# A first expert's tokens gathered as a transposed product, with bias products and tables in other places

## The reference, cut to what matters

```python
h = layer_norm(DEEPNORM_ALPHA * h + t, ln_g[i, 0], ln_b[i, 0])
# moe_ffn(h):
logits = (xt @ w_router + b_router).astype(jnp.float32)
top_logit, top_e = lax.top_k(logits, TOP_K)          # 4 of 32 experts
gate = jax.nn.softmax(top_logit, axis=-1)
...
h = xb @ w_gu[e] + b_gu[e]                           # per expert, on its tokens
h_gate, h_up = jnp.split(h, 2, axis=-1)
act = h_gate * jax.nn.sigmoid(SWIGLU_ALPHA * h_gate) * (h_up + 1.0)
return act @ w_down[e] + b_down[e]
```

## Time and profile before

| | us |
|---|---|
| runs of the kernel | 1381.45, 1381.24, 1382.12 |
| the profiled execution's own time | 1380.81 |
| its span, first to last instruction | 1379.0 |
| PE busy | 1334.6 |
| DVE busy | 441.3 |
| ACT busy | 346.8 |
| mean granted TensorE clock | 0.990 |

### The profile page before, as it was taken

The page is one execution under the profiler, slowest core; times in us unless marked ns, Lnnn a source line. Parts: engine busy times, 40 slices in busy tenths (PEclk is TensorE's granted clock), DMA queues, the critical chain, the costliest instruction groups (busy, mean ns, idle before and its releaser), DMA issues.

```text
span 1379.0 us, 17054 instructions
## 1 busy us (share of the span) xinstructions
PE 1334.6 (97%) x7358; PEld 719.0 (52%) x7358; DVE 441.3 (32%) x746; ACT 346.8 (25%) x576; POOL 48.6 (4%) x58
## 2 busy tenths in 40 slices
PE   9999999999999999969999999999999999999997
PEld 7996333333333333313333333333336998999986
DVE  5565121111111111011111110111116776878853
ACT  4441011101101110000011010110116545666642
POOL 2010000000000000000000000000002000022200
PEclk9999999999999999979999999999999999999999
DMA  9768999999999999999999999999996444265530
GB/s 376 315 236 356 424 423 429 431 430 431 430 431 430 431 430 431 431 430 429 431 431 431 429 431 432 430 429 432 430 428 271 153 153 153 79 258 184 184 122 31
DMA packets 44346, 484.17 MB, mean 351 GB/s; under 512 B 4748, under 2 KB 4800, under 8 KB 13680
## 3 DMA queue, kind: packets, MB, share of 16 engines
q1 hardware_dynamic: 42432, 477.63, 83.2%
q0 software_dynamic: 1840, 5.44, 1.1%
HBM read 481.99 MB, written 1.06 MB: 350 GB/s over the span
## 4 chain that ended last, share of the span: by engine, by line
PE 83%; DMA 11%; DVE 3%; issue 1%; ACT 1%; DVEq 0%; SPq 0%; ACTq 0%
PE bank L832 27%; PE bank L638 18%; PE bank L840 13%; DMA ring<-in_moe_w_gate_up 8%; PE bank L1140 4%; PE bank L852 4%; PE bank L805 4%; PE bank L621 3%; PE bank L824 2%; DMA ring<-in_w_in 2%; PE bank L748 2%; PE bank L1076 1%; PE bank L1026 1%; DMA arena<-in_x_by_feature 1%; DVE w_split L1549 1%
## 5 line engine op out<-in xcount | busy, mean ns | idle before, releaser
L832 PE MATMUL bank<-ring,arena 128*64 128x512 f32 x2032 | 448.2, 597 | 9.7 <-DMA ring<-in_moe_w_gate_up 9.6
L832 PEld LDWEIGHTS bank<-ring,arena 128*64 128x64 f32 x2032 | 142.5, 137 | 314.0 <-issue 291.2
L1747 DVE TENSOR_SCALAR arena<-bank 128x512 f32<-128x512 f32 x32 | 22.1, 692 | 658.6 <-PE bank L832 658.6
L840 PE MATMUL bank<-ring,arena 128*64 128x512 f32 x1024 | 227.0, 595 | 2.4 <-DMA ring<-in_moe_w_down 2.0
L638 PE MATMUL bank<-x_hi,w_split 128*128 128x256 f32 x1056 | 193.7, 284 | 2.1 <-DVE x_lo L1556 2.1
L638 PEld LDWEIGHTS bank<-x_hi,w_split 128*128 128x128 f32 x1056 | 165.9, 192 | 2.6 <-DVE x_lo L1556 1.5
L1549 DVE TENSOR_TENSOR w_split<-ring,w_split 128x2048 fp32r<-128x2048 f32 x61 | 139.5, 2290 | 60.3 <-ACT w_split L1195 60.1
L638 PE MATMUL bank<-x_lo,w_split 128*128 128x256 f32 x528 | 149.4, 283 | 0.0
L1296 ACT ACTIVATE arena<-arena 128x512 f32<-128x512 f32 x32 | 20.2, 630 | 498.8 <-DVE arena L1747 498.8
L840 PEld LDWEIGHTS bank<-ring,arena 128*64 128x64 f32 x1024 | 70.8, 137 | 137.9 <-issue 128.8
L1195 ACT CAST w_split<-ring 128x2048 fp32r<-128x2048 f32 x62 | 118.2, 1909 | 74.0 <-PE bank L638 42.5
(11 more groups left out here) (292 smaller groups left out, 1104.5 us busy)
## 6 DMA issues: line engine op xcount, KB each, us to landing
ring<-in_moe_w_gate_up SPq DMA_DIRECT2D x127, 2048.0 KB, 29.3
ring<-in_moe_w_down SPq DMA_DIRECT2D x64, 2048.0 KB, 30.3
ring<-in_ffn_w_up SPq DMA_DIRECT2D x22, 1024.0 KB, 4.8
ring<-in_w_in SPq DMA_DIRECT2D x14, 1024.0 KB, 8.1
ring<-in_ffn_w_down SPq DMA_DIRECT2D x11, 1024.0 KB, 4.8
ring<-in_a_w_in SPq DMA_DIRECT2D x10, 1024.0 KB, 20.8
ring<-in_a_w_out SPq DMA_DIRECT2D x2, 2048.0 KB, 13.8
ring<-in_w_out SPq DMA_DIRECT2D x4, 1024.0 KB, 5.0
```

What stands on the lines that cost most here:

```text
L832: last = mm(bank[q // 2][half * 64:half * 64 + 64, :], chunk(xeT, c), w[:, c % 2, q * 512:(q + 1) * 512], start=False, stop=c == KC - 1)
L840: last = mm(bank[3][half * 64:half * 64 + 64, :], chunk(actT, c), w[:, c % 4, half * 512:(half + 1) * 512], start=c == 0, stop=c == KC - 1)
```

## The change

- OUT_BANKS puts one half of the attention output in bank 7 instead of bank 0; the router's and the rank counts' results move to banks 4 and 5. Banks 0 and 1 are then free early.
- `add_bias` of the first expert runs right behind the first tile's router product. `bias_sel` for it is made before the layer norm.
- h1 is written and announced in halves of 512 columns.
- The first expert's tokens are gathered with h1 as the stationary operand (`gather_first`): eight products 64 columns wide for each tile, whose result is already transposed. The first copy of ACT and the four transposes go. The part of tile 0 runs when tile 0 is chosen and ranked, that of tile 1 after its own choice.
- The table transposes (`tables`) move behind the first weight piece.
- Of the four fillers behind the first router product one is left, and one of 256 columns is new.

```diff
-        OUT_BANKS = (4, 6, 5, 0)
+        OUT_BANKS = (4, 6, 5, 7)
...
+            def gather_first(t):
+
+                for c in range(KC):
+                    start = c // 2 * 256 + c % 2
+                    last = mm(bank[2][:, c % 4 * P + c // 4 * 64:c % 4 * P + c // 4 * 64 + 64], h1[:, t, start:start + 255:2],
+                              sel[:, t, :], start=t == 0 and c == 0, stop=t == NT - 1, skip_group_check=True)
+                return last
+
             for t in range(NT):
-                pe.wait_ge(h1_ready, t + 1)
                 for g in range(2):
+                    pe.wait_ge(h1_ready, 2 * t + g + 1)
...
                 if t:
+                    pe.wait_ge(chosen_ready, 1)
+                    mm(RANKS[0], before, chosen[:, 0, :], start=True, stop=True).then_inc(rank_ps, 1)
+                    pe.wait_ge(h1T_dve, 1)
+                else:
                     repeat(3, 1)
-                    pe.wait_ge(h1T_dve, 1)
+                    pe.wait_ge(moe_small_in, 4 * 16)
...
                 if t == 0:
+                    pe.wait_ge(bsel_ready, 1)
+                    add_bias()
                     repeat(3, 1)
 
-            pe.wait_ge(chosen_ready, 1)
-            mm(bank[0][:, 0:N_EXP], before, chosen[:, 0, :], start=True, stop=True)
-            mm(bank[0][:, N_EXP:2 * N_EXP], ones, chosen[:, 0, :], start=True, stop=False)
-            repeat(3, 1)
+            pe.wait_ge(sel_ready, 1)
+            gather_first(0)
+            mm(bank[3][:, 0:T], ident, cst[:, 0:T], start=True, stop=True)
+            mm(RANKS[1], ones, chosen[:, 0, :], start=True, stop=False)
             pe.wait_ge(chosen_ready, 2)
...
-            repeat(3, 1)
+            mm(RANKS[1], before, chosen[:, 1, :], start=False, stop=True).then_inc(rank_ps, 1)
+            pe.wait_ge(sel_ready, 2)
+            gather_first(1).then_inc(xeT_ps, 1)
...
-            pe.wait_ge(sel_ready, 1)
-            gather().then_inc(xe_ps, 1)
...
-            pe.wait_ge(xe_ready, 1)
-            turn_chunks(2, xe, 2).then_inc(xeT_ps, 1)
...
                     gate_up(s, buffer_of(n, 2)).then_inc(piece_done, 1)
+                    if i == 0 and s == 0:
+                        tables()
...
-            act.wait_ge(xe_ps, 1)
-            copy(xe, bank[2][:, :]).then_inc(xe_ready, 1)
...
+                for g in range(2):
+                    cols = slice(g * 512, (g + 1) * 512)
+                    stt(h1[:, t, cols], h1[:, t, cols], r, row_b[:, cols], ALU.mult, ALU.add).then_inc(h1_ready, 1)
+            places = const("slot")
+
+            def first_places(t):
+
+                dve.wait_ge(rank_ps, t + 1)
+                link(stt(place[:, t, :], RANKS[t], 0.5, chosen[:, t, :], ALU.add, ALU.mult))
+                ts(sel[:, t, :], places[:, 0:CAP], place[:, t, 0:1], None, ALU.is_equal).then_inc(sel_ready, 1)
```

More of the change, by code:

```diff
@@ L164, in build @@
         LEVEL_BANKS = (4, 6, 7, 4, 5, 6, 7, 4)
-        OUT_BANKS = (4, 6, 5, 0)
+        OUT_BANKS = (4, 6, 5, 7)
+        LOGITS = [bank[4][:, t * N_EXP:(t + 1) * N_EXP] for t in range(NT)]
+        RANKS = [bank[5][:, t * N_EXP:(t + 1) * N_EXP] for t in range(NT)]
         OUT_ORDER = (3, 0, 1, 2)
@@ L191, in build @@
         selgT = at(3456, NT, P)
-        bias_sel = at(3712, CAP, rows=64)
+        bias_sel = at(13548, CAP, rows=64)
         actT = at(6144, 4, P)
@@ L772, in _, with add_bias @@
             before = const("before")
+            def add_bias():
+                for half in range(2):
+                    for q in range(2):
+                        rows = slice(q * 32, q * 32 + 32)
+                        mm(bank[q][half * 64:half * 64 + 64, :], bias_sel[rows, :], bgu[rows, half, :],
+                           start=True, stop=False)
+            def gather_first(t):
[4 more added lines that the diff above has]
+                return last
             for t in range(NT):
-                pe.wait_ge(h1_ready, t + 1)
                 for g in range(2):
+                    pe.wait_ge(h1_ready, 2 * t + g + 1)
                     b = 4 + 2 * t + g
@@ L818, in chunk @@
                 return v[:, c % 4, (c // 4) * 64:(c // 4) * 64 + 64]
[L820 to L825, removed]
             def gate_up(s, w):
@@ L854, in scatter, with tables @@
                 return last
-            pe.wait_ge(sel_ready, 1)
-            gather().then_inc(xe_ps, 1)
[L858 to L861, removed]
-                turn(bank[3][0:N_EXP, T + t * P:T + (t + 1) * P], place[:, t, :])
-            for t in range(NT):
-                last = mm(bank[4][0:N_EXP, 0:1], chosen[:, t, :], ones[:, 0:1], start=t == 0, stop=t == NT - 1)
-            last.then_inc(table_ps, 1)
-            pe.wait_ge(xe_ready, 1)
-            turn_chunks(2, xe, 2).then_inc(xeT_ps, 1)
+            def tables():
+                pe.wait_ge(gates_ready, 1)
+                for t in range(NT):
+                    turn(bank[3][0:N_EXP, t * P:(t + 1) * P], gates[:, t, :])
+                for t in range(NT):
+                    turn(bank[3][0:N_EXP, T + t * P:T + (t + 1) * P], place[:, t, :])
+                for t in range(NT):
+                    last = mm(bank[4][0:N_EXP, 0:1], chosen[:, t, :], ones[:, 0:1], start=t == 0, stop=t == NT - 1)
+                last.then_inc(table_ps, 1)
             def put_down(i):
@@ L1653, in choose @@
                 dve.wait_ge(logit_ps, t + 1)
-                link(tt(logit[:, t, :], bank[1 + t][:, 0:N_EXP], br, ALU.add))
+                link(tt(logit[:, t, :], LOGITS[t], br, ALU.add))
                 link(dve.max(top8[:, t, :], logit[:, t, :]))
@@ L1664, in choose, with select_bias @@
                                   ALU.add).then_inc(chosen_ready, 1)
+            def select_bias(i):
+                ts(bias_sel, ones[0:64, 0:CAP], const("own")[0:64, i:i + 1], None, ALU.mult).then_inc(bsel_ready, 1)
+            select_bias(0)
             for t in range(NT):
@@ L1676, in _ @@
                 r = refine(t)
-                stt(h1[:, t, :], h1[:, t, :], r, row_b, ALU.mult, ALU.add).then_inc(h1_ready, 1)
+                for g in range(2):
[6 more added lines that the diff above has]
+                ts(sel[:, t, :], places[:, 0:CAP], place[:, t, 0:1], None, ALU.is_equal).then_inc(sel_ready, 1)
             choose(0)
@@ L1680, in _ @@
             dve.tensor_copy(h1T[:, 4:8, P:T], bank[7][:, :].rearrange("p (c n) -> p c n", c=4)).then_inc(h1T_dve, 1)
+            first_places(0)
             choose(1)
             dve.wait_ge(chosen_ready, 2)
-            places = const("slot")
+            first_places(1)
             def select(i):
@@ L1688, in select @@
                    place[:, :, i:i + 1].to_broadcast([P, NT, CAP]), ALU.is_equal).then_inc(sel_ready, 1)
-            def select_bias(i):
-                ts(bias_sel, ones[0:64, 0:CAP], const("own")[0:64, i:i + 1], None, ALU.mult).then_inc(bsel_ready, 1)
             def weigh(i):
@@ L1697, in weigh @@
                 last.then_inc(selg_ready, 1)
-            dve.wait_ge(rank_ps, 1)
-            link(stt(place.rearrange("p t e -> p (t e)"), bank[0][:, 0:2 * N_EXP], 0.5,
-                chosen.rearrange("p t e -> p (t e)"), ALU.add, ALU.mult))
-            select(0)
             dve.wait_ge(gexp_ready, 1)
@@ L1732, in _ @@
                 if i + 1 < N_EXP and not pause:
-                    dve.wait_ge(xe_ps, i + 1)
+                    dve.wait_ge(*((xe_ps, i) if i else (xeT_ps, 1)))
                     select(i + 1)
```

24 lines of the change are left out of this document (10 added, 14 removed).

## The result

The changed kernel takes 1385.51 us (median of 7 runs, 1383.07 to 1386.85), the kernel before 1381.38 (7 runs, 1380.89 to 1382.83). The ratio is 1.0026, 95% interval [1.0017, 1.0036]: 4.1 us slower, 0.3%. The forecast was 1387.0 with a range of 1380.2 to 1390.5.

What follows compares the result with a forecast made beforehand. The full DMA stream of weights, whose head waits for PE, was taken as the bound. The middle, +5.6, of +7.4 and +3.7 on 1380.81 gave 1386.4, and 0.6 for the runs 1387.0; range 1380.2 to 1390.5.

Steps and rivals of the forecast that it cites:

- What bounds the kernel: MoE: the full DMA weight stream sets the end; its head waits for PE's first weight piece, us for us.
- The room: Stream's head: piece 11 lands 8.1 us after issue, a lone piece 7.5, so 0.6 us of lateness is free.
- 1.5 us of room cover it: Tables behind the first weight piece: 0.8 us of PE, covered by piece 20's landing 9.0 after issue against 7.5.
- Up to the clock's fall nothing moves.: PE up to tile 0's router product: same list as before, so the clock falls as before, at about 119.2.
- a later fall: Clock falls at 125, behind tile 1's router product: first weight piece done at 141.0, +4.3, stream +3.7.
- the middle, +5.6: End of the kernel: the forecast taken between +7.4 (early fall) and +3.7 (later fall).
- The first branch: Clock falls at about 119.2 and stays at 1.2 GHz well into the expert products: piece +8.0, stream +7.4.
- The upper end of the range: 1390.5 us: the early fall with the narrow products at double price, +8.6, and 0.6 for the runs.
- The narrow products at 1.2 GHz: Router product and gather_first on PE: 3.2 us per sixteen instead of 1.80, by the transposes' ratio 1.81 / 1.03.
- The rival that they keep their time: Narrow products bound by loads do not slow with the clock: +3.2 or 1.0, 1382.5 to 1384.7; chance 0.10.
- The strides: gather_first loads h1 with a stride of two: at most 0.9 us more per batch of 16, taken as 0.
- The gain of an early first piece: Stream's head: an earlier first weight piece only closes the dip from 360 to 430 GB/s, at most 0.8 us.

Runs made afterwards that it cites:

- a_hotlate: a_hot with the tables behind the third weight piece of the first expert instead of the first: 1382.03 us, ratio 0.9992.
- b_nofill: The kernel before without its two fillers around the rank products: 1382.74 us, ratio 1.0017.
- b_delay: The kernel before with five more fillers of 512 columns ahead of the first expert's gather: 1385.29 us, ratio 1.0031.
- b_narrow: The kernel before with both gather_first in place of the old gather, ACT's copy and the transposes, nothing else: 1382.76 us, ratio 1.0007.
- b_first: The kernel before with one more filler, ahead of tile 0's router product: 1381.44 us, ratio 1.0005.
- a_again: The changed kernel once more, unaltered: 1385.84 us, ratio 1.0025 to the kernel before.
- a_nofirst: The changed kernel without its filler ahead of tile 0's router product: 1387.33 us, ratio 1.005 to the kernel before.
- a_fill: The changed kernel with three full fillers where PE would wait, one replacing the 256-column one: 1383.98 us, ratio 1.0024 to the kernel before.
- a_wide: The changed kernel with the old wide gather, ACT's copy and four transposes instead of both gather_first: 1384.76 us, ratio 1.0022 to the kernel before.
- a_hot: a_fill plus a full filler ahead of gather_first(0) and a 256-column one ahead of tile 1's router product: 1381.86 us, ratio 1.001.
- a_latetab: The changed kernel with the tables behind the first expert's third weight piece instead of the first: 1384.88 us, ratio 1.0018 to the kernel before.
- a_midlate: a_hotlate without the 256-column filler ahead of tile 1's router product: 1383.19 us, ratio 1.0012 to the kernel before.

## Why the prediction was right

Right in its result and mostly in its mechanism; one premise and two sizes were wrong.

**What bounds the kernel.** Right. Over the 14 profiled executions the second layer's first load is issued a nearly fixed time behind piece 12: 869.03 us in the kernel before (1009.18 less 140.15), and 868.8 to 869.6 in all but one. The exception is a_hotlate at 870.95, whose piece 11 took 10.0 us to land, and the trace doesn't show why. So up to that load what counts is when PE releases the slots of pieces 11 and 12. From its issue to the end of the execution it was 370.7 to 372.3 us, and 372.9 to 373.3 in the four executions with the fall in the second layer. In the table all times are in us, and the lateness is against the kernel before.

| profiled execution | filler ahead of tile 0's router product | clock at 1.2 GHz, 115 to 145 | piece 11 late | second layer's first load late |
|---|---|---|---|---|
| kernel before | no | 119.2 to 122.6 | | |
| b_nofill | no | 127.7 to 131.1 | 0.84 | 0.95 |
| b_delay | no | 125.7 to 129.2 | 4.88 | 4.74 |
| b_narrow | no | never | 0.48 | 0.34 |
| b_first | yes | 125.1 to 128.5 | 0.22 | 0.27 |
| changed kernel | yes | 126.2 to 139.9 | 4.05 | 5.12 |
| a_again | yes | 126.4 to 140.1 | 3.99 | 4.68 |
| a_nofirst | no | 120.3 to 123.8, 127.2 to 140.8 | 5.57 | 6.63 |
| a_fill | yes | never | -1.05 | 0.35 |
| a_wide | yes | 120.5 to 124.0, 127.4 to 141.0 | 5.32 | 6.75 |
| a_hot | yes | never | 0.05 | 1.34 |
| a_latetab | yes | 126.7 to 140.4 | 4.26 | 4.52 |
| a_hotlate | yes | 122.1 to 125.5 | 2.67 | 4.59 |
| a_midlate | yes | 125.8 to 142.9 | 8.04 | 8.41 |

**The room.** The prediction took 0.6 us of room at piece 11 and 1.5 us for the tables. Both came from comparing a landing time with that of a lone piece, 7.5 us. That holds for the first late piece only. The piece behind it lands 9.1 to 9.3 after its issue in all the kernels whose stream had run dry (9.3 after, 9.1 in b_delay and b_nofill); the piece ahead had not landed when it was issued (148.26 against 145.10 after). In the kernel before piece 12 took 9.5 (140.15 to 149.65): by that its room was 0.2 to 0.4, and in the loads not even this is to be seen, as they are as late as piece 12 within about 0.5 in all traces but a_hotlate's. The tables, placed exactly ahead of it, cost their 0.9. The step "1.5 us of room cover it" failed, because it looked at piece 20. The 0.8 named there as their price past the cover was close.

**"Up to the clock's fall nothing moves."** This step failed twice. A filler had been added ahead of tile 0's router product, so the list was not the same. And the place of the fall does not repeat even where it is: b_nofill, b_delay and b_narrow have the kernel before's own list up to 125, and their clock fell at 127.7, at 125.7 and never. Of the five executions without the filler two have an early fall, of the nine with it a_wide and a_hotlate. So the traces don't show that the filler put it off. The prediction was a middle of two branches, +7.4 and +3.7. The changed kernel is the second, "a later fall": issue of piece 11 predicted at 141.0, measured 140.76; stream +3.7, measured +5.1: the tables add 0.9, the missing room 0.6, a piece 11 a little earlier than forecast takes 0.25 off, and the rest is open. Even the 141.0 is in part two errors that cancel: the second `gather_first` started at 129.96, about 1.1 earlier than the sum has it, as the clock fell only inside the first, and from there to the end of the weight piece it took about 0.9 more. That the middle, +5.6, came close to +4.1 to +4.9 is partly luck: the branch that took place, with the room and the tables as forecast, gives 1385.1, and the two terms that it lacks happen to be about what the middle adds. The first branch, one fall from 119 into the expert products, is in no trace: where the clock fell that early, in four executions, it was back after 3.4 to 3.5 us. The upper end of the range does not follow from its terms either: 1380.81 + 8.6 + 0.6 is 1390.0, not 1390.5.

**The narrow products at 1.2 GHz.** The forecast was 3.2 us for sixteen, measured 3.68 with the end of the last one. From their start to the next instruction's, as the 1.80 was read that it comes from, they took 3.31 in a_midlate (134.01 to 137.32). Their weight loads, by groups at 2.4 and at 1.2 GHz:

```profile
L808 PEld LDWEIGHTS bank<-arena 128*128 128x128 f32 x16 | 1.9, 191 | 0.8 <-issue 0.8
...
L788 PEld LDWEIGHTS bank<-arena 128*128 128x128 f32 x16 | 3.5, 328 | 0.8 <-DVE arena L1705 0.8
```

The mean load goes from 191 to 328 ns, a ratio of 1.72 beside the 1.76 of the transposes. The rival that they keep their time falls. By the rule quoted from the Trainium skill ("TensorE: Matmul & The Clock Gate", LDWEIGHTS) such a load would take 107 ns, an estimate from its 128 columns, with no word of the clock. The trace disagrees at both clocks.

**The strides.** Taken at 0, and nothing more is to be seen: at 2.4 GHz in a_fill sixteen strided products took 1.92 us from their start to the next instruction's (125.00 to 126.92), in the same trace sixteen contiguous ones, half as wide, 1.87 (117.44 to 119.31).

**The gain of an early first piece.** It was capped at 0.8. In a_fill piece 11 went out 1.05 early, the stream ran at 436 instead of 360 GB/s from 135 to 140 and at 397 instead of 442 from 140 to 145, with piece 12 held back by the tables. Piece 12 went out at 140.00, 0.15 early, and the second layer's first load was not earlier (1009.53). So an early piece 11 gave nothing in this execution, while piece 12 was not early too.

**Why the clock stays down.** That fillers can give the loss back is shown: a_hot, with five more and all the other edits in place, keeps the clock in its profiled execution and gives back 3.3 of the 4.65 us of the median. Three (a_fill) and four (a_midlate, with its tables late) gave back less, 2.0 and 2.65, with more spread. The kernel before does with fewer, so their number alone isn't the cause. The moved bias products and tables left waits bare as well, and no run moves them back alone, so their share isn't separated from the fillers'. That the narrow gather does it, as the experiments first assumed, is refuted: a_wide has none and loses as much, b_narrow has it and kept the clock. What the traces have in common is only argued. The short falls, 3.4 us each, had fillers, transposes or the wide gather running behind them. In the changed kernel, a_wide and a_midlate, what followed the long fall was broken by waits or mixed with narrow products, and the clock came back only 3 to 6 us into the expert products. Against this reading stands the wide gather: in b_nofill the clock was back at its end, in a_wide it ran unbroken for 3.68 us and the clock stayed down. So what decides whether an execution has a fall, and how long it lasts, is open: in a_midlate, one and the same program, five runs of twelve are longer by 5 us or more.

## What to carry to other kernels

An instruction whose result nobody reads can be what carries the time. Before work is moved into a gap or taken out of one, look which waits it leaves bare and what the granted clock does there, and compare the instruction lists whole, row by row. A transfer's spare time is its landing time less that of a piece issued in the same situation, behind another late one, and not less that of a lone one. And where the granted clock decides, one profile is one draw: look at every run's time and at several profiles, and ask of each fall whether anything on the chain that ended last stood under it. The mean clock over the whole span is a weak guide, as a fall in a place with spare time lowers it and costs nothing.

## What the runs showed of the hardware that was not expected

- One program, two outcomes: a_midlate's runs form two groups 5 us apart or more (1380.3 to 1383.4 and 1388.6 to 1390.4), whose mean granted clocks do not overlap (0.992 to 0.996 and 0.985 to 0.989).
- In a_midlate's profile the granted clock stayed at 1.2 GHz for 16.6 us in which PE was busy for 16.60, with weight loads and narrow products among its work.
- The place of a fall is not the program's alone: the kernel before, b_nofill, b_delay and b_narrow have the same list of instructions up to 125, and the clock fell at 119.2 in the first and not before 125 in the other three.
- A fall of 3.4 us cost 1.5 us where PE was on the chain that ended last (26.18 and 27.67 us for the same 216 products), and nothing measurable in b_first.
- Full fillers took 0.95 us each at 2.4 GHz and 1.85 at 1.2. In the profiles, piece 11 was issued at 144.75 with four full ones and the clock down (a_midlate), and at 140.76 in the changed kernel: fillers that fail to hold the clock make it worse.
